# The first microseconds of an FP32 transformer kernel: x loaded in halves on ScalarE's queue, the first two weight pieces split row by row, constants loaded behind them

## What is computed

```python
def rmsnorm(x, g):
    y = x * lax.rsqrt(jnp.mean(x * x, axis=-1, keepdims=True) + NORM_EPS)
    return y * g
def swiglu(h, w_gu, w_down):
    gate, up = jnp.split(h @ w_gu, 2, axis=-1)
    return (jax.nn.silu(gate) * up) @ w_down
# first of all, D_MODEL = 1024, D_FF = 2816:
x = x + 0.5 * swiglu(rmsnorm(x, ffn1_norm[0]), ffn1_w_gu[0], ffn1_w_down[0])
...
```

## Time and profile before

| | |
|---|---|
| median of 3 runs | 3012.59 us (3011.95 to 3013.51) |
| the profiled execution, its time | 3011.13 us |
| its span in the profile | 3009.3 us |
| TensorE busy (PE) | 2906.3 us, 97% of the span |
| VectorE busy (DVE) | 1823.5 us, 61% |
| ScalarE busy (ACT) | 1597.6 us, 53% |
| GpSimd busy (POOL) | 117.6 us, 4% |
| DMA, all 16 engines | 575.08 MB, mean 191 GB/s |
| TensorE's granted clock, mean | 0.993 |

### The profile page before, as it was taken

One profiled execution on the slowest core, in us unless ns is written; L12 is line 12 of the kernel. 1 busy time (PEld: TensorE's weight loads), 2 busy tenths in 40 slices (PEclk: granted clock), 3 DMA queues, 4 the chain that ended last, 5 costly groups with the idle time before them and its releaser, 6 DMA issues. The chain is left out here.

```text
span 3009.3 us, 36498 instructions
## 1 busy us (share of the span) xinstructions
PE 2906.3 (97%) x14562; PEld 2458.2 (82%) x14562; DVE 1823.5 (61%) x2206; ACT 1597.6 (53%) x2014; POOL 117.6 (4%) x104
## 2 busy tenths in 40 slices
PE   7999899999999999989999998999999999999998
PEld 6888788888988888868888887878888787888776
DVE  4558565565665555586555585555575655675664
ACT  4447764454454454555454476644476453565452
POOL 0003300000000000000000024000000000000000
PEclk9999999999999999999999999999999999999999
DMA  7764247677547767537767742277545585645674
GB/s 232 218 208 142 70 140 223 225 215 240 175 153 225 231 210 236 190 99 222 231 209 215 220 140 98 85 237 234 179 152 181 191 268 198 200 153 182 208 246 161
DMA packets 447594, 575.08 MB, mean 191 GB/s; under 512 B 19744, under 2 KB 301472, under 8 KB 447424
## 3 DMA queue, kind: packets, MB, share of 16 engines
q1 hardware_dynamic: 447424, 572.74, 60.6%
HBM read 540.16 MB, written 32.51 MB: 190 GB/s over the span
## 5 line engine op out<-in xcount | busy, mean ns | idle before, releaser
L630 DVE TENSOR_TENSOR lo<-raw,hi 128x2048 fp32r<-128x2048 f32 (+1 forms) x479 | 1075.1, 2254 | 822.8 <-ACT hi L612 822.0
L612 ACT ACTIVATE hi<-raw 128x2048 fp32r<-128x2048 f32 (+2 forms) x489 | 912.6, 1871 | 868.8 <-DMA raw<-in_ffn_w_gu 400.3
L426 PE MATMUL ps<-hi,xh 128*128 128x512 f32 (+1 forms) x2208 | 864.5, 392 | 4.7 <-DVE lo L630 2.4
L428 PE MATMUL ps<-hi,xl 128*128 128x512 f32 (+1 forms) x2208 | 858.7, 389 | 0.0
L427 PE MATMUL ps<-lo,xh 128*128 128x512 f32 (+1 forms) x2208 | 858.5, 389 | 0.0
L426 PEld LDWEIGHTS ps<-hi,xh 128*128 128x128 f32 x2208 | 415.3, 188 | 91.6 <-DVE lo L630 5.6
L428 PEld LDWEIGHTS ps<-hi,xl 128*128 128x128 f32 x2208 | 415.2, 188 | 85.4
L427 PEld LDWEIGHTS ps<-lo,xh 128*128 128x128 f32 x2208 | 415.5, 188 | 83.5
L426 PE MATMUL ps<-hi,hhh 128*128 128x512 f32 x704 | 276.4, 393 | 5.4 <-DVE hhl L951 4.7
L427 PE MATMUL ps<-lo,hhh 128*128 128x512 f32 x704 | 275.1, 391 | 0.0
L428 PE MATMUL ps<-hi,hhl 128*128 128x512 f32 x704 | 275.0, 391 | 0.0
(11 more groups left out here) (434 smaller groups left out, 3119.1 us busy)
## 6 DMA issues: line engine op xcount, KB each, us to landing
raw<-in_ffn_w_gu SPq DMA_DIRECT2D x352, 512.0 KB, 5.2
raw<-in_ffn_w_down SPq DMA_DIRECT2D x80, 1024.0 KB, 6.6
raw<-in_w_ff SPq DMA_DIRECT2D x64, 1024.0 KB, 7.1
raw<-in_w_in SPq DMA_DIRECT2D x60, 1024.0 KB, 5.2
raw<-in_gdn_w_in SPq DMA_DIRECT2D x32, 1024.0 KB, 5.8
turned<-hhf SPq DMA_DIRECT2D x88, 256.0 KB, 2.4
hhr<-turned SPq DMA_DIRECT2D x352, 64.0 KB, 5.8
raw<-in_sb_w_in SPq DMA_DIRECT2D x12, 1024.0 KB, 5.1
```

Source lines behind the costliest of these rows:

```text
L426: e.matmul(o, a1, r1, start=kk == 0, stop=False)
L428: i = e.matmul(o, a2, r1, start=False, stop=kk == kts - 1)
L612: k.e.activation(k.m.hi[q % RING][:, 0:n], k.m.raw[q % RING][:, 0:n], ACT.Copy).then_inc(*k.up("act_piece_hi", ("hi", q)))
L630: k.e.tensor_tensor(m.lo[i][:, 0:n], m.raw[i][:, 0:n], m.hi[i][:, 0:n].bitcast(F32), ALU.subtract).then_inc(*k.up("dve_piece_lo", ("split" ...
```

## The change

SP's order at the begin becomes: the identity alone (64 KB), half of piece 0, the gains alone, the rest of pieces 0 and 1 in halves of two rows (`sync_fine`), piece 2, and only then the constants, the other vector columns and the rows, then pieces 3 and 4. ScalarE issues x itself, as four DMAs (half of the positions by half of the features), ahead of its first work. ScalarE and VectorE split pieces 0 and 1 row by row, alternating a row's split with a block of xh or xl (`scalar_start`, `vector_start`), and TensorE waits per row (`split`, p, j). x's transposes take a PSUM bank for each feature block. TensorE transposes the identity 9 times before x and 4 times after its first half, into a bank that nobody reads (`tensor_warm`). The squares and the norm's factor move behind the splits of pieces 2 and 3 (`squares`), and the first feed-forward stage gets a script of its own. In the diff below, blank lines and some lines of context are left out, and most of the new script.

```diff
@@ -19,6 +19,7 @@
 AHEAD = 3
+FINE = 2
 PIECE = 2048
@@ -345,7 +346,7 @@
     def due(self, p):
-        at = lambda p: min(len(self.pieces), p + 1 + min(AHEAD, p + 1)) if p >= 0 else 1
+        at = lambda p: max(FINE, min(len(self.pieces), p + 1 + min(AHEAD, p + 1)))
         return range(at(p - 1), at(p))
     def steps(self, p):
@@ -413,7 +414,7 @@
                     k.wait_ge(*b.before)
-                k.wait_ge("split", p)
+                k.wait_ge(*(("split", p, j) if p < FINE else ("split", p)))
                 for event in ready(kk, t):
@@ -546,7 +547,29 @@
 def tensor_x1(k, si):
+    if not si.g:
+        return tensor_first_x(k, 1)
     return tensor_turn_kept(k, si.g, 1) if si.before else tensor_turn_x(k, si.g, 1)
+def turned_at(g, c):
+    first = c if not g else c // 2 * 2
+    return first, slice((c - first) * S, (c - first + 1) * S)
+def tensor_first_x(k, s):
+    for c in range(4 * s, 4 * s + 4):
+        b = k.take("xT", 0, c)
+        k.wait_ge(*b.before)
+        for t in range(2):
+            k.wait_ge("x", 0, t, s)
+            i = k.e.transpose(b.ps[:, t * P:(t + 1) * P], k.m.x[:, t, c * P:(c + 1) * P], k.m.C(C_ID))
+        i.then_inc(*k.up("pe_x_turned", ("xT", 0, c)))
+        k.close(b)
+    yield
 def tensor_turn_x(k, g, s):
@@ -649,15 +672,35 @@
+def scalar_xh(k, si, c):
+    first, part = turned_at(si.g, c)
+    m, b = k.m, k.bank("xT", si.g, first)
+    k.wait_ge("xT", si.g, first)
+    k.e.activation(m.xh[:, c, :], b.ps[:, part], ACT.Copy, scale=m.col(si.gain + c)).then_inc(
+        *k.up("act_xh", ("xh", si.g, c)))
+def scalar_start(k, plan, si):
+    for s in range(2):
+        for r in range(2):
+            k.e.dma_start(k.m.x[:, r, 512 * s:512 * s + 512], k.t["x"][0, r * P:(r + 1) * P, 512 * s:512 * s + 512]).then_inc(
+                *k.up(f"dma_x{2 * s + r}", ("x", 0, r, s), ("res", 0, r, s), by=16))
+    for c in range(8):
+        q, j = c // 4, c % 4
+        k.wait_ge("landed", q, j // 2)
+        k.e.activation(k.m.hi[q][:, 512 * j:512 * j + 512], k.m.raw[q][:, 512 * j:512 * j + 512], ACT.Copy).then_inc(
+            *k.up("act_piece_hi", ("hi", q, j)))
+        k.wait_ge("gains")
+        scalar_xh(k, si, c)
 def scalar_turned_x(k, si, s):
-    e, m, g = k.e, k.m, si.g
-    for a in (4 * s, 4 * s + 2):
-        b = k.bank("xT", g, a)
-        k.wait_ge("xT", g, a)
-        for j in range(2):
-            e.activation(m.xh[:, a + j, :], b.ps[:, j * S:(j + 1) * S], ACT.Copy, scale=m.col(si.gain + a + j)).then_inc(
-                *k.up("act_xh", ("xh", g, a + j)))
+    g = si.g
+    for c in range(4 * s, 4 * s + 4):
+        scalar_xh(k, si, c)
     scalar_squares(k, g, s)
@@ -679,7 +722,8 @@
 def scalar_x1(k, si):
-    return scalar_turned_kept(k, si.g, 1) if si.before else scalar_turned_x(k, si, 1)
+    return iter((None,)) if not si.g else scalar_turned_kept(k, si.g, 1) if si.before else scalar_turned_x(k, si, 1)
 def scalar_squares(k, g, s):
@@ -699,22 +743,57 @@
+def scalar_first_rstd(k):
+    scalar_squares(k, 0, 0)
+    yield
+    scalar_squares(k, 0, 1)
+    yield
+    k.wait_ge("const")
+    scalar_rstd(k, 0)
+    yield
+def vector_first_rstd(k):
+    yield
+    yield
+    vector_sumsq(k, 0)
+    yield
 def vector_sumsq(k, g):
+def vector_xl(k, si, c):
+    first, part = turned_at(si.g, c)
+    m, g, b = k.m, si.g, k.bank("xT", si.g, first)
+    k.wait_ge("xh", g, c if not g else first + 1)
+    k.e.scalar_tensor_tensor(m.xl[:, c, :], b.ps[:, part], m.col(si.gain + c), m.xh[:, c, :].bitcast(F32), ALU.mult, ALU.subtract).then_inc(
+        *k.up("dve_xl", ("xl", g, c), *([b.read] if c % 2 or not g else [])))
+def vector_start(k, plan, si):
+    m = k.m
+    for c in range(8):
+        q, j = c // 4, c % 4
+        part = slice(512 * j, 512 * j + 512)
+        k.wait_ge("hi", q, j)
+        k.e.tensor_tensor(m.lo[q][:, part], m.raw[q][:, part], m.hi[q][:, part].bitcast(F32), ALU.subtract).then_inc(
+            *k.up("dve_piece_lo", ("split", q, j)))
+        k.wait_ge("gains")
+        vector_xl(k, si, c)
 def vector_turned_x(k, si, s):
-    e, m, g = k.e, k.m, si.g
-    for a in (4 * s, 4 * s + 2):
-        b = k.bank("xT", g, a)
-        k.wait_ge("xh", g, a + 1)
-        for j in range(2):
-            c, i = a + j, b.ps[:, j * S:(j + 1) * S]
-            e.scalar_tensor_tensor(m.xl[:, c, :], i, m.col(si.gain + c), m.xh[:, c, :].bitcast(F32), ALU.mult, ALU.subtract).then_inc(
-                *k.up("dve_xl", ("xl", g, c), *([b.read] if j else [])))
+    g = si.g
+    for c in range(4 * s, 4 * s + 4):
+        vector_xl(k, si, c)
     if s == 1:
@@ -958,6 +1037,13 @@
+FFN_FIRST_SCRIPT = """
+W x1 W squares W squares squares gate flip W W gate W send W send W W fetch flip gate fetch W turn flip W gate
...
+"""
 FFN_SCRIPT = """
@@ -1006,6 +1092,7 @@
     run(script, {"W": scalar_pieces(k, plan, g), "x1": scalar_x1(k, si), "gate": gate(), "turn": scalar_flipped(k, r["f"], g),
+                 **({} if g else {"squares": scalar_first_rstd(k)}),
                  "norm": scalar_norm(k, si), "next": scalar_next(k, nxt)})
@@ -2848,30 +2936,43 @@
+def tensor_warm(k, b, n, *events):
+    for _ in range(n):
+        i = k.e.transpose(b.ps[:, 0:P], k.m.C(C_ID), k.m.C(C_ID))
+    i.then_inc(*k.up("pe_warm", *events))
 def tensor_program(k, plan, infos):
-    k.wait_ge("const")
-    run(["x0"], {"x0": tensor_turn_x(k, 0, 0)})
+    b = k.take("warm")
+    k.wait_ge("id")
+    tensor_warm(k, b, 9)
+    for _ in tensor_first_x(k, 0):
+        pass
+    tensor_warm(k, b, 4, b.read)
+    k.close(b)
     for si, nxt in zip(infos, infos[1:]):
+        if si.g == 1:
+            k.wait_ge("const")
         TENSOR[si.name](k, plan, si, nxt, SCRIPT[si.name](plan, si))
 def scalar_program(k, plan, infos):
-    scalar_split(k, plan, 0)
-    k.wait_ge("const")
-    run(["x0"], {"x0": scalar_turned_x(k, infos[0], 0)})
+    scalar_start(k, plan, infos[0])
     for si, nxt in zip(infos, infos[1:]):
 def vector_program(k, plan, infos):
-    vector_split(k, plan, 0)
+    vector_start(k, plan, infos[0])
+    for si, nxt in zip(infos, infos[1:]):
+        if si.g == 1:
+            k.wait_ge("const")
+        VECTOR[si.name](k, plan, si, nxt, SCRIPT[si.name](plan, si))
+def pool_program(k, plan, infos):
     k.wait_ge("const")
-    run(["x0"], {"x0": vector_turned_x(k, infos[0], 0)})
-    for si, nxt in zip(infos, infos[1:]):
-        VECTOR[si.name](k, plan, si, nxt, SCRIPT[si.name](plan, si))
-def pool_program(k, plan, infos):
     for si, nxt in zip(infos, infos[1:]):
@@ -2885,6 +2986,15 @@
             *k.up(f"dma_ring{p % RING}", *([("landed", p)] if n == len(parts) - 1 else []), by=16))
+def sync_fine(k, plan, p, h):
+    dims, parts = plan.pieces[p]
+    view = k.m.ring(k.m.raw, p, dims)
+    for n, (index, src) in enumerate(parts):
+        k.e.dma_start(view[:, 2 * h:2 * h + 2, n], src[:, 2 * h:2 * h + 2]).then_inc(
+            *k.up(f"dma_fine{2 * p + h}", *([("landed", p, h)] if n == len(parts) - 1 else []), by=16))
 def sync_gains(k, si):
@@ -2930,13 +3040,17 @@
 def sync_program(k, plan, infos, out):
     e, m, t = k.e, k.m, k.t
-    sync_piece(k, plan, 0)
-    e.dma_start(m.const[:, :], t["consts"]).then_inc(*k.up("dma_const", by=16))
-    e.dma_start(m.vec[:, :], t["vecs"]).then_inc(*k.up("dma_const", by=16))
-    e.dma_start(m.row[:, :], t["rows"].partition_broadcast(P)).then_inc(*k.up("dma_const", by=16))
-    x = [(n, 0, r, s) for n in ("x", "res") for r in range(2) for s in range(2)]
-    e.dma_start(m.x[:, :, :], t["x"][0].rearrange("(t p) d -> p t d", p=P)).then_inc(*k.up("dma_const", ("const",), *x, by=16))
-    for p in range(1, RING):
+    e.dma_start(m.const[:, 0:P], t["consts"][:, 0:P]).then_inc(*k.up("dma_id", ("id",), by=16))
+    sync_fine(k, plan, 0, 0)
+    e.dma_start(m.vec[:, 0:V_CONV], t["vecs"][:, 0:V_CONV]).then_inc(*k.up("dma_gains", ("gains",), by=16))
+    sync_fine(k, plan, 0, 1)
+    for h in range(2):
+        sync_fine(k, plan, 1, h)
+    sync_piece(k, plan, 2)
+    e.dma_start(m.const[:, P:], t["consts"][:, P:]).then_inc(*k.up("dma_const", by=16))
+    e.dma_start(m.vec[:, V_CONV:], t["vecs"][:, V_CONV:]).then_inc(*k.up("dma_const", by=16))
+    e.dma_start(m.row[:, :], t["rows"].partition_broadcast(P)).then_inc(*k.up("dma_const", ("const",), by=16))
+    for p in range(3, RING):
         sync_piece(k, plan, p)
```

More of the change, by code:

```diff
@@ L737, in vector_x1 @@
 def vector_x1(k, si):
-    return vector_turned_kept(k, si.g, 1) if si.before else vector_turned_x(k, si, 1)
+    return iter((None,)) if not si.g else vector_turned_kept(k, si.g, 1) if si.before else vector_turned_x(k, si, 1)
 def vector_out(k, si, half, keep=None):
@@ L958, in ffn_room @@
     return dict(f=Flips(m, r, "hh", 11, 2, 2, 3), sg=[r(f"sg{i}", [P, 256]) for i in range(4)])
+FFN_FIRST_SCRIPT = """
+W x1 W squares W squares squares gate flip W W gate W send W send W W fetch flip gate fetch W turn flip W gate
```

(8 more changed lines are left out.)

## The result

The changed kernel takes 2999.47 us, the median of 6 runs (2994.96 to 3002.42), against 3011.56 for the kernel before in 6 runs. The ratio is 0.9962, with a 95% interval from 0.9949 to 0.9976: 7 to 15 us faster. The profiled execution takes 3001.02 us, with a span of 2999.2, 10.1 us less than in the profile of before. I forecast 3003.3 (2998.5 to 3008.0), faster: right, near the fast end of the range.

A forecast was written before the change was run, and what follows sets the result against it. TensorE, busy 97% of the span, was taken as the bound, so time is won only where it idles or runs slowly. Begin 8.8 plus script 0.5 gave 9.3 us: 3003.3 us for the median, range 2998.5 to 3008.0.

The forecast's parts named there:

- First product: At the kernel's begin: TensorE's first product starts at 8.6 us instead of 17.07, bounds 7.6 and 10.5.
- the landing of the half piece: At the begin: x's first half, half a piece, identity and gains, 1.16 MB, all land at about 6.9 us.
- Clock and piece 2: First eight rows: 12 products at half clock take 5.25 us, and piece 2 starts at 23.5 us instead of 32.30.
- Piece 4: First stage: ScalarE's chain behind piece 3 ends in time, so piece 4 starts at 34.4 us without a wait, 8.8 won.
- The new script: First stage: 4.3 us of end losses go, a 2.1 us wait at piece 14 costs 3.8 in all; net 0.5 won.
- a difference of over 1 us: Behind the first stage: any difference of more than 1 us there would prove the prediction wrong.
- The first (no wait): At piece 14: no wait, so all of 4.3 us is won, 13.1 in sum, 2999.5 us; chance 0.25.
- The second: At the begin: the pieces win over x, first product at 10.5 us, piece 4 at 36.0, 3004.9 us; chance 0.12.
- The third: First stage: piece 14 waits 3 us and the last chunk still waits 1.9, 4.8 won, 3007.8 us; chance 0.09.
- The fourth (SP behind flips): First stage: sends waiting for flips hold later loads, 3.8 us each; at six places slower by 9.7, 3022.3 us; chance 0.03.
- The fifth: At the begin: x's place gains nothing, first product at 13.2 us, piece 4 at 38.6, 3007.5 us; chance 0.06.
- The sixth: At the begin: the clock rises before the first product, only 0.2 us kept, 3003.1 us; chance 0.45 together with the forecast.

The follow-up runs named there:

- e8: e5 with x's second half loaded by SP behind the first half of piece 0 and the gains; ratio 0.9939 against the kernel before, 0.9942 when run again.
- e9: e8 with 9 + 10 transposes of the identity instead of 9 + 4; ratio 0.9942 against the kernel before.
- after_again: The changed kernel, unchanged, with one more profile and more timed rounds; ratio 0.9962 against the kernel before.
- e4: The changed kernel with the send of chunk 4 moved behind the loads of piece 14; ratio 0.9954 against the kernel before.
- e2: The changed kernel with 1 + 1 transposes of the identity instead of 9 + 4; ratio 0.9970 against the kernel before.
- e7: The kernel before with only the first stage's new script, its squares left out; ratio 1.0001 against the kernel before.
- e1: The changed kernel with the old script's order in the first feed-forward stage; ratio 0.9981 against the kernel before.
- e3: The changed kernel with x's four DMAs issued by SP behind the identity instead of by ScalarE; ratio 0.9977 against the kernel before.
- e5: e4 with piece 3 loaded by SP ahead of the constants instead of behind them; ratio 0.9955 against the kernel before.
- e6: The changed kernel with pieces 0 and 1 split whole instead of row by row, all loads unchanged; ratio 0.9990 against the kernel before.

## Why the prediction was right, and where not

- **First product: 8.6 forecast, 9.63 measured** (9.48 again). The step that failed is the landing of the half piece: 6.9 forecast, 7.73 measured (7.58 again); the chain behind it took 1.9 us, not 1.7. I had x's first half and the half piece end together, and counted 1.16 MB. But ScalarE issues both halves of x at once, and x's second half (0.52 MB) was in no term of the sum. e8 moves it behind the half piece, and this lands at 6.57 and 6.21 (6.27 in e9), ahead of all six profiles that have the changed kernel's loads ahead of it (7.22 to 9.40). The rule of the Trainium skill cited in the prediction (DMA: Bandwidth & Descriptors, Issuing engines are not separate DMA queues) agrees: loads of two issuers compete. Why x's first half was there 1.7 us before the half piece is not shown.
- **Clock and piece 2.** I let the clock rise as late as before. In the changed kernel it was up by the first product; in after_again too, but fell for 7 products. Piece 2 came at 21.69 and 23.12, against 23.5.
- **Piece 4: 34.4 forecast, 33.66 and 34.15 measured.** The chain behind piece 3 is there (0.80 us of waiting in the first profile, none in the second, where TensorE was late itself), with piece 3 split from 21.91 instead of 22.7. Gain 9.7 and 9.0 against 8.8.
- **The new script: 0.5 us forecast.** The wait at piece 14 was foreseen in place and cause, but mis-sized: 4.30 us (3.40 again) instead of 2.1, and above my bound of 3; with the half clock behind it, it cost about 6 us (e4) instead of 3.8. From the end of chunk 3 at about 55.4 to lo of piece 14 at 92.4 the links took 37 us, not 34.7, the fetch 3.08 instead of 2.3, the landings 6.6, 4.1 and 3.9. The end's waits vanished as forecast. In the changed kernel's first profile the script's exchange came out at 2.0 us of loss (stretch 166.6 against 164.6), about what before differs from itself by (1.7).
- **Sum.** By the profiles' stage ends, 7.7 and 10.4 us (first with first, second with second), mean 9.05, against 9.3 forecast; timed 11.4 (0.38%), interval 7.2 to 15.4. The begin won more than its term (9.7 and 9.0 against 8.8), the script less (2.0 us lost in the first pair, 1.4 won in the second). That the sum fits this well is in part luck: a second profile of either kernel moved its stage end by 1.3 to 1.5 us, and 2.4 us of the first profile's gain lie behind the stage. There I had named a difference of over 1 us as a sign of being wrong; it was no fit sign, as the kernel before differs from itself by 4.6 us there.
- **Rivals.** The first (no wait) is what e4 made. The second has it the wrong way round: x was there before the half piece. The third fell, as the waits at the stage's end are gone. The fourth (SP behind flips) happened once, at 6 us and not in four places. The fifth fell. The sixth came about, in after_again with only transposes run before, and made little difference at piece 4 (0.6 us against e2, or 0.1 by after_again).

## What to carry to other kernels

At a program's begin, sum the bytes ahead of the first operation on all queues together, load what it needs in the size in which it is used, and put everything else behind; then look which of its inputs lands last: here half a megabyte of x, moved behind the half piece, let the half piece land 1.0 to 1.5 us earlier. In a queue that runs in order, a send that waits for a late result should stand behind the loads whose buffers are already free: here one such send cost 6 us, more than half of what the early begin had won. A loop slower than the engine that sets the time uses up that engine's lead, so a gain at the begin has to be followed to the end of the stage.

## What the runs showed of the hardware

- **The clock after a wait.** After 4.30 us of idle TensorE ran at a granted clock of 0.50 to about 97.4 us; after 1.94 us in e7 and 1.90 us in e1 it stayed at 1.00, while 1.89 us in the profile of before and 1.89 us in after_again's begin were followed by 0.50. Waits of nearly the same length went both ways; the longer ones at the begin (3.46 us in e3, 3.50 in e5, 7.95 in e6) were all followed by 0.50.
- **The clock at the begin** came up at very different points behind the same 9 + 8 + 4 transposes: before 7 us in after_again, between the last transpose and the first product (8.6 to 9.6 us) in the changed kernel, and only at about 13.3 us in e1. Transposes alone are enough for it to rise: in after_again nothing else had run.
- **Landing times scatter.** The first half piece, with the same loads ahead of it, landed at 7.22 to 9.40 us in e1, e2, e4, e5 and the changed kernel's two profiles; five of the six lie within 0.5 us.
- **Chips and executions differ** by about as much as the change is worth (11.4 us): the kernel before had a median of 3008.2, 2999.5 and 3010.3 us in three sets of runs, and single runs of one set lay up to 15 us apart. Only ratios within a set tell anything here.
